# A slot's weighted sum in four 64x64 quarters of the array instead of four full-array products

## The reference

```
act = gelu(u . h) * g          # one number for each token and slot
out = sum over the 128 slots of act * v
```

## Time and profile before

| | |
|---|---|
| median of 3 runs | 2990.7 us (2988.2 to 2991.11) |
| span of the profiled execution | 2989.7 us |
| PE busy | 2666.7 us, 89% |
| weight loads (beside PE) | 2186.6 us, 73% |
| DVE busy | 2159.7 us, 72% |
| ACT busy | 637.2 us, 21% |
| POOL busy | 990.5 us, 33% |
| DMA | 1182.34 MB, mean 395 GB/s |

### The profile page before, as it was taken

One profiled execution on the slowest core, in us unless ns is written; L12 is line 12 of the kernel. 1 busy time (PEld: TensorE's weight loads), 2 busy tenths in 40 slices (PEclk: granted clock), 3 DMA queues, 4 the chain that ended last, 5 costly groups with the idle time before them and its releaser, 6 DMA issues.

```text
span 2989.7 us, 35028 instructions
## 1 busy us (share of the span) xinstructions
PE 2666.7 (89%) x11992; PEld 2186.6 (73%) x11992; DVE 2159.7 (72%) x6678; ACT 637.2 (21%) x1699; POOL 990.5 (33%) x1028
## 2 busy tenths in 40 slices
PE   8999999899998888989998888989999887877787
PEld 6778888678887677877887776868787665555555
DVE  1248858787588978687688778778588777678565
ACT  3231311272113116101111215201211110102001
POOL 0013333333333333333333333333333343333332
PEclk9999999999999999999999999999999999999999
DMA  5369999999999999999999999999999999999998
GB/s 190 103 247 426 413 408 426 426 365 409 415 387 392 386 427 405 425 421 427 426 415 416 414 426 416 413 427 423 427 398 407 409 427 426 426 417 411 427 425 344
DMA packets 166802, 1182.34 MB, mean 395 GB/s; under 512 B 19408, under 2 KB 19936, under 8 KB 24032
## 3 DMA queue, kind: packets, MB, share of 16 engines
q0 software_dynamic: 147456, 1073.81, 86.8%
q1 hardware_dynamic: 19168, 106.31, 9.0%
HBM read 1177.95 MB, written 2.10 MB: 395 GB/s over the span
## 4 chain that ended last, share of the span: by engine, by line
PE 53%; DMA 26%; DVE 11%; issue 8%; ACT 1%; POOL 0%; DVEq 0%; SPq 0%; POOLq 0%; ACTq 0%
PE main_bank L337 35%; DMA main_ring<-in_uv,main_idi 26%; PE main_bank L375 9%; PE main_bank L373 5%; DVE main_diagonal L311 2%; DVE main_ring L297 1%; DVE main_pick L202 1%; PE main_bank L543 1%; DVE main_hid L297 1%; DVE main_idf L209 1%; DVE main_topi L162 1%; DVE main_work L154 1%; DVE main_pick L196 1%; PE main_bank L735 1%; DVE main_topi L156 1%
## 5 line engine op out<-in xcount | busy, mean ns | idle before, releaser
L337 PE MATMUL main_bank<-main_ring,main_diagonal 128*128 128x256 f32 (+1 forms) x8160 | 1989.8, 390 | 294.6 <-DVE main_diagonal L311 294.0
L337 PEld LDWEIGHTS main_bank<-main_ring,main_diagonal 128*128 128x128 f32 x8160 | 1536.7, 193 | 656.4 <-DVE main_diagonal L311 434.4
L297 DVE CUSTOM_DVE_ANT_0 main_ring<-main_ring,main_bank 128x1024 f32<-128x1024 f32 x1024 | 1247.8, 1219 | 619.6 <-DMA main_ring<-in_uv,main_idi 607.0
L280 POOL DMA_INDIRECT main_ring<-in_uv,main_idi x1024 | 990.3, 967 | 1977.8 <-PE main_bank L337 1751.1
L302 ACT ACTIVATE main_act_out<-main_hid 128x1 f32<-128x1 f32 x1024 | 206.5, 203 | 2164.8 <-DVE main_hid L297 2153.5
L311 DVE TENSOR_SCALAR main_diagonal<-main_ident,main_act_out,main_gate 128x128 f32<-128x128 f32 x1024 | 359.2, 351 | 21.0 <-ACT main_act_out L302 13.9
L375 PE MATMUL main_bank<-main_xT,main_w_block 128*128 128x256 f32 x1408 | 358.4, 381 | 1.9 <-ACT main_xT L408 1.9
L375 PEld LDWEIGHTS main_bank<-main_xT,main_w_block 128*128 128x128 f32 x1408 | 268.3, 191 | 38.9 <-ACT main_xT L408 2.3
L375 PE MATMUL main_bank<-main_xT_query,main_w_block 128*128 128x256 f32 x512 | 124.2, 379 | 0.9 <-ACT main_xT_query L408 0.9
L375 PEld LDWEIGHTS main_bank<-main_xT_query,main_w_block 128*128 128x128 f32 x512 | 96.6, 190 | 14.5 <-ACT main_xT_query L408 1.2
L302 ACT ACT_TABLE_LOAD x82 | 105.2, 1283 | 1.4
(11 more groups left out here) (196 smaller groups left out, 1206.7 us busy)
## 6 DMA issues: line engine op xcount, KB each, us to landing
main_w_block<-in_w_query SPq DMA_DIRECT2D x32, 1024.0 KB
main_w_block<-in_w_ab SPq DMA_DIRECT2D x24, 1024.0 KB
main_ring<-in_uv,main_idi POOLq DMA_INDIRECT x1024
main_w_block<-in_w_c_in SPq DMA_DIRECT2D x16, 1024.0 KB
main_w_block<-in_w_out SPq DMA_DIRECT2D x8, 1024.0 KB
main_w_block<-in_w_c_out SPq DMA_DIRECT2D x8, 1024.0 KB
main_att_bias<-in_att_bias SPq DMA_DIRECT2D x16, 256.0 KB
main_keys<-in_keysT SPq DMA_DIRECT2D x2, 1024.0 KB, 12.8
```

Of the source, the lines that this page charges most:

```text
L280: nc.gpsimd.indirect_dma_start(self.ring[n % self.bufs], None, self.uv[p // NT], bass.IndirectOffsetOnAxis(self.choice.idi[:, p % 2, k:k + ...
L297: self.nc.vector.tensor_tensor_reduce(out=row, in0=row, in1=self.ps[:, 6:8], scale=1.0, scalar=0.0, op0=ALU.mult, op1=ALU.add, accum_out=s ...
L337: last = self.nc.tensor.matmul(self.ps[:, 4 + at // T, at % T:at % T + wide], self.diagonal[:, n % DIAGS], self.ring[n % self.bufs][:, D + ...
```

## The change

A slot's v rows (128 partitions x 1024 columns) are taken as four quarters: rows r = 0, 1 (partitions 0 to 63, 64 to 127) by column halves a = 0, 1. Each is one product with a 64x64 diagonal and 512 moving columns, on the quarter of the array that belongs to input partitions r and output partitions a. So the sum for rows r and columns a stands in bank 4 + r, on partitions 64a to 64a + 63. The diagonal matrix is [128, 64] (the identity of 64 twice, one below the other, loaded from HBM as a new constant), and `place` makes 64 columns. Because the sums now stand on other partitions than the residual rows, `add` takes four instructions of 64 partitions x 512 columns in place of one. The last tile's halves take two each.

```diff
-        self.diagonal = room.sb("diagonal", [P, DIAGS, P])
+        self.diagonal = room.sb("diagonal", [P, DIAGS, SIDE])      # SIDE = P // 2
...
-        self.nc.vector.tensor_scalar(self.diagonal[:, n % DIAGS], self.ident[:], self.act_out[:, k:k + 1],
+        self.nc.vector.tensor_scalar(self.diagonal[:, n % DIAGS], self.ones[:], self.act_out[:, k:k + 1],
...
     def add(self, dve, p):
         dve.wait_ge(self.v_done, (p + 1) * HK)
-        rows = self.resid[:, p % NT].rearrange("p (a d) -> p a d", a=2)
-        self.nc.vector.tensor_tensor(rows, self.ps[:, 4:6], rows, ALU.add).then_inc(self.added, 1)
+        for a in range(2):
+            last = self.add_columns(p, a)
+        last.then_inc(self.added, 1)
         dve.wait_ge(self.added, p + 1)
+
+    def add_columns(self, p, a):
+
+        cols = slice(a * T, (a + 1) * T)
+        for r in range(2):
+            rows = self.resid[r * SIDE:(r + 1) * SIDE, p % NT, cols]
+            last = self.nc.vector.tensor_tensor(rows, self.ps[a * SIDE:(a + 1) * SIDE, 4 + r], rows, ALU.add)
+        return last
...
-            half = self.resid[:, NT - 1, a * T:(a + 1) * T]
-            self.nc.vector.tensor_tensor(half, self.ps[:, 4 + a], half, ALU.add).then_inc(self.half_added, 1)
+            self.add_columns(2 * NT - 1, a).then_inc(self.half_added, 1)
...
-        wide = T if k == 0 else BC
-        for a in range(D // wide):
-            at = a * wide
-            last = self.nc.tensor.matmul(self.ps[:, 4 + at // T, at % T:at % T + wide], self.diagonal[:, n % DIAGS],
-                                         self.ring[n % self.bufs][:, D + at:D + at + wide], start=k == 0, stop=k == HK - 1 and at % T + wide == T)
-            if n == 2 * NT * HK - 1 and at + wide == T:
+        for a in range(2):
+            for r in range(2):
+                rows = slice(r * SIDE, (r + 1) * SIDE)
+                last = self.nc.tensor.matmul(self.ps[a * SIDE:(a + 1) * SIDE, 4 + r], self.diagonal[rows, n % DIAGS],
+                                             self.ring[n % self.bufs][rows, D + a * T:D + (a + 1) * T], start=k == 0, stop=k == HK - 1)
+            if n == 2 * NT * HK - 1 and a == 0:
                 last.then_inc(self.half_done, 1)
         last.then_inc(self.v_done, 1)
...
+            sp.dma_start(diagonal[:], A["diagonal"]).then_inc(loaded[1], 16)
...
-            act.wait_ge(loaded[1], 32)
+            act.wait_ge(loaded[1], 48)
...
-            dve.wait_ge(loaded[1], 32)
+            dve.wait_ge(loaded[1], 48)
```

More of the change, by code:

```diff
@@ L82, in block @@
         return self.stack.enter_context(self.nc.Block())
-ROOM = 48312
 BUFS = 7
@@ L90 @@
 HALF = T // 2
+SIDE = P // 2
+ROOM = 48312 - DIAGS * SIDE
 class Room:
@@ L257, in __init__ @@
     def __init__(self, nc, s, choice, A, consts, bank, resid, scale, gain_rows, ring, room):
-        self.nc, self.choice, self.ident, self.ps, self.resid, self.scale = nc, choice, consts["ident"], bank, resid, scale
+        self.nc, self.choice, self.ones, self.ps, self.resid, self.scale = nc, choice, consts["diagonal"], bank, resid, scale
         self.uv, self.gain, self.ring = (A["uv0"], A["uv1"]), gain_rows, ring
@@ L1277, in trunk @@
         iota = s.sb("iota", [P, P])
-        consts = {"ident": ident, "iota": iota}
+        diagonal = s.sb("ones", [P, SIDE])
+        consts = {"ident": ident, "iota": iota, "diagonal": diagonal}
         bank = s.ps("bank", [P, 8, T])
@@ L1758 @@
         "ident": np.eye(P, dtype=np.float32),
+        "diagonal": np.tile(np.eye(SIDE, dtype=np.float32), (2, 1)),
         "iota": np.arange(P, dtype=np.float32),
```

## The result

The changed kernel takes 2970.4 us (median of 4, 2967.0 to 2973.1) against 2990.9: ratio 0.9934, 95% interval 0.9920 to 0.9948. It is faster by 20 us where 40 were forecast: inside the range, but half the size. The change is clear of the measurement's noise, the intervals reaching some 4 us to either side. Measured again in a later set it gave 0.9930 (0.9916 to 0.9943). The profiled execution of the first set has a span of 2965.1 us, granted clock 0.857 (before: 2989.7 and 0.985); it is the fastest of the four, so this pair of profiles shows 4 us more gain than the medians. A second profile of the changed kernel, from the later set, has a span of 2972.2 us.

The account below looks back on a forecast made before the run. DMA's top rate of 427 GB/s was taken as the bound, with 73 us lost under it; 43 us come back, less 3 for the adds, so 2989.7 - 40 = 2950 of span, plus 1.0: 2951 us, range 2915 to 2984.

Parts of the forecast that it names:

- What bounds the kernel: Whole kernel: transfers set the pace at 427 GB/s; only time under that rate, 73 us, can be won.
- the floor of 2917: Whole kernel: even an infinitely fast TensorE gives no less than about 2917 us.
- The products: TensorE, each slot: four quarters together stream 0.86 us instead of 1.73; a pair of switches costs 0.42 us.
- passes in order: Rival, 4%: TensorE starts records in order, so a slot stays at 1.73 us and switches come on top: 3079 us.
- The clock: TensorE: falls in tiles 6 and 7 cost nothing; rival, 6%: also low where products are mixed in, 3074 us.
- place: VectorE, each slot: making 64 diagonal columns takes 284 ns instead of 351, 67 ns less, 69 us of its time.
- The end: Last two slots and last adds: 4.8 us against 4.43, so 0.4 us later.
- The sum: All tiles: shares of each tile's gap come back, together 43 us, less 3 for the adds: 40 us.
- the DVE rival: Rival, 9%: VectorE's bursts, not TensorE, make the gaps in tiles 1, 3 and 5, so little is won: 2982 us.
- the 415 that I named: Tile 1: a DMA rate of 415 GB/s or more would show the forecast right.
- my sign of being wrong: Tile 1 staying under 405 GB/s with PE below 90%, or L337's records following one another 0.43 us apart.
- The adds: VectorE, tile boundaries: four adds cost 1.6 us more, 7 times, 11 us; 3 us of it charged.

Follow-up runs that it names:

- the filler: Changed kernel with four zero-weight quarter products behind each slot of tiles 1 to 7 that has no other product behind it: 2968.9 us, ratio 0.9936.
- The square: Kernel before and changed kernel, each with and without the choice of experts for tiles 2 to 7: 2990.9 and 2965.0 us before, 2970.4 and 2949.1 us changed.

## Why the prediction was half right

- **What bounds the kernel: right.** The top of 427 GB/s held in every run, and the floor of 2917 was not touched, not even with a sixth of VectorE's work gone (2141.0 us busy to 1792.7, 2949.1 us).
- **The products: right.** 0.86 us streamed a slot, a lone slot 1.09 us, 0.38 us for a pair of switches against 0.42. The rival "passes in order" is out by the 1.09. Two quarters at a time, whose slot streams 1.73 us, gave 3083 where that rival had 3079: its total was right, in part by luck, since tiles 2 and 4, which it charged nothing, lost 15 us more.
- **The clock: the fall was right (0.69 in tiles 6 and 7) and its rival is out.** It also fell where products are mixed in: to 0.90 or 0.91 in tiles 1, 3 and 5, over the 0.86 from which I had put the damage, and to 0.86 and 0.85 in tiles 2 and 4, at that mark. Those two tiles got longer by no more than 1 us in either profile, and the filler shows no cost above 4 us in the whole.
- **place: mis-sized.** 30 ns less, not 67: the nearest form reads from PSUM, and its fixed part and its price for 64 columns are others. What 30 ns are worth is at most 4 us, and nothing that was measured.
- **The end: mis-sized.** From the last diagonal to the last add I forecast 0.4 us more; it was 6.1 us (2953.76 to 2959.86 below) against 4.5, 1.6 in place of 0.4 more. From 2954.25 on the granted clock was 0.5, so most of the two last slots ran at the half clock: 3.25 us and not 2.0.

```profile
2953.76 3.25 PE main_bank L344 x14
2957.01 0.02 issue
2957.03 0.68 DVE main_resid L325
...
2959.15 0.71 DVE main_resid L325
```

- **The step that failed is in "The sum": the shares of each tile's gap that I gave to TensorE by how busy it was.** "Tiles 3 and 5 (92%) half of 14.1 = 7", "tile 2 ... 40% of 11.7 = 5", "tile 4 40%", "tiles 6 and 7 half" came to 18 us; those tiles gave 5 in one profile and 3 in the other. The square shows why: with the choice left out, tile 3 ran at 426 GB/s on a TensorE 94% busy. An engine that busy and not late anywhere held nothing. What held tiles 3 and 5, and over half of tile 2, was VectorE's choice, in bursts of some 3 to 5 us of work between two dots; what held tile 4 and the rest of tile 2 stays open. I had the DVE rival for all tiles at once or for none, and misread a row for it: its "DVE's 90% in the stretch above" was 74.0 of 90 us, 82%; only after the change is it 91%. It was true tile by tile, and the result lies between its 2982 and my 2951.
- **The same step in tile 1, which gave 16 and 11 us of the 20.** One share of 70% for the whole tile hid that it has two parts. Behind the attention, 13 of 16 us came back, over 70%. In its first 48 slots, with PE at 124 of 137 us, the loss went from 12.4 to 9.9 and 14.6: nothing. So the tile stood at 411 and 406 GB/s, under the 415 that I named, though over the 405 of my sign of being wrong. What is left lies in 560 to 690, the attention:

```profile
560.00:690.00 130.00, 99.01 (x584) 41.26 (x588) 113.00 (x366) 73.12 (x133) 44.02 (x46) 0.85 0.98 395
```

  130 x (1 - 395 / 427) = 9.7 us, with PE at 76%. The changed kernel's waits there name ScalarE's softmax twice, and VectorE's diagonal between them:

```profile
PEld main_bank L750 <- ACT main_att_p L841: 28.5, 15, 3.4
PEld main_bank L344 <- DVE main_diagonal L310: 25.7, 17, 4.0
PE main_bank L750 <- ACT main_att_pT L851: 14.8, 13, 2.6
```

  In PE's program the slots stand behind the attention's products, so that a late product makes the next slot late. VectorE is the rival, at 113 of 130 us. Taking the diagonal off VectorE and putting it on ScalarE made the first 48 slots worse in both kernels (18.7 us lost before the change, 18.6 after it), which speaks for ScalarE; a kernel without the attention's waits was not run, so this part is argued, not shown.
- **The adds: open.** I charged 3 us of 11. Taking 10.7 us off showed no gain, within 4 us.
- **What is still lost** in the changed kernel, 55 us by the table: some 8 stand at the end, as the prediction has it, 16 are VectorE's choices, 13 to 17 lie in tile 1. Tiles 2 and 4 lose 5 each without choices; the recurrent mixer's bursts are my guess, and no run took them away.

## What to carry to other kernels

Where a transfer sets the pace, measure each stage by what it loses against the top rate, and ask of each engine not how busy it is but whether it is ever late: in tile 3 TensorE at 93% held nothing, and in tile 2 VectorE at 77% held over half of what was lost, through bursts of 3 to 6 us between two dots that the ring of buffers could not bridge. Cut a stage where its work changes: the part of tile 1 with the attention and the part without it answered to different things. Leaving out one engine's side work in both versions (a square of four runs) gives the shares that busy times cannot. And quarters of the array halved the time of a slot's fp32 products (1.73 us of streaming to 0.86) only with all four streaming; with two at a time, the switches to the full array cost 92 us in the whole.

## What the runs showed of the hardware that was not expected

- An fp32 scalar product of a constant tile with two numbers of each partition takes 351 ns for 128 columns and 321 for 64: 64 columns cost 30 ns. Two other forms pay twice as much for 64: tensor-by-scalar instructions that read PSUM by 65 (284 ns for 64 columns, 479 for 256, in the kernel before), an add by 66 (692 ns for 512, 1223 for 1024).
- An add of 64 partitions x 512 takes 688 ns (the changed kernel's), one of 128 x 512 692 (the one before's): half the partitions save nothing.
- On ScalarE a one-column copy scaled by a number of each partition takes 294 ns, the gelu of one column 202 and the copy of 64 columns, scaled so, 348 (the version with the diagonal on ScalarE).
- Products with zero weights keep the granted clock up: with four of them behind each slot it stood at 0.98 in tile 6, without them at 0.68.
- The DMA engines' busy share doesn't tell the rate: 0.99 of the time at 397 GB/s in the kernel before (tile 1 behind its attention), 1.01 at 427 in tile 6.
